# GpSimd subtracts four weight tiles at a time in place of two, from the fourth slot on

## What is computed

```python
proj = jnp.einsum('bsd,de->bse', h.astype(w_in.dtype), w_in)              # input projections
... mixers ...
return jnp.einsum('bse,ed->bsd', mix.astype(w_out.dtype), w_out)          # output projections
return (jax.nn.silu(h @ w_gate) * (h @ w_up)) @ w_down                    # feed-forward
```

## Time and profile before

| | |
|---|---|
| runs | 1914.07, 1914.70, 1916.35 us |
| profiled execution, first to last instruction | 1915.6 us |
| TensorE busy | 1770.9 us, 92% |
| VectorE busy | 926.6 us, 48% |
| ScalarE busy | 758.6 us, 40% |
| GpSimd busy | 950.2 us, 50%, of which the splits (L2811) 813.6 us |
| mean granted TensorE clock | 0.966 of full speed |

### The profile page before, as it was taken

One profiled execution on the slowest core, in us unless ns is written; L12 is line 12 of the kernel. 1 busy time (PEld: TensorE's weight loads), 2 busy tenths in 40 slices (PEclk: granted clock), 3 DMA queues, 4 the chain that ended last, 5 costly groups with the idle time before them and its releaser, 6 DMA issues.

```text
span 1915.6 us, 20168 instructions
## 1 busy us (share of the span) xinstructions
PE 1770.9 (92%) x7526; PEld 1337.8 (70%) x7526; DVE 926.6 (48%) x1394; ACT 758.6 (40%) x1261; POOL 950.2 (50%) x1108
## 2 busy tenths in 40 slices
PE   9999989999989889789999999998889899999996
PEld 6766557677767666466888888865445678888885
DVE  2043435666836799526632413357547544032344
ACT  4264554365464324644332322343333542222231
POOL 4433124457944454024655556569124456565662
PEclk9999999999999999799999999999879999999998
DMA  5221112222102221012322332311001223333231
GB/s 201 86 64 61 33 45 87 66 67 77 56 23 88 66 77 56 2 54 89 95 94 97 100 99 93 97 54 55 11 12 33 67 69 96 99 99 98 90 99 66
DMA packets 39697, 139.90 MB, mean 73 GB/s; under 512 B 4528, under 2 KB 4656, under 8 KB 39472
## 3 DMA queue, kind: packets, MB, share of 16 engines
q1 hardware_dynamic: 39600, 138.61, 22.6%
HBM read 136.50 MB, written 2.10 MB: 72 GB/s over the span
## 4 chain that ended last, share of the span: by engine, by line
PE 76%; DVE 11%; ACT 7%; POOL 3%; issue 2%; DMA 0%; SPq 0%; ACTq 0%; DVEq 0%; POOLq 0%
PE ps L643 18%; PE ps L645 17%; PE ps L644 17%; DVE ps L1882 2%; PE ps L706 2%; PE ps L683 2%; POOL wl L2811 2%; PE ps L685 2%; PE ps L684 2%; PE ps L663 1%; PE ps L669 1%; PE ps L660 1%; PE ps L1281 1%; PE ps L959 1%; ACT wh L741 1%
## 5 line engine op out<-in xcount | busy, mean ns | idle before, releaser
L2811 POOL TENSOR_TENSOR wl<-raw,wh 128x256 fp32r<-128x256 f32 x988 | 813.6, 854 | 842.0 <-ACT wh L741 836.3
L741 ACT ACTIVATE wh<-raw 128x1024 fp32r<-128x1024 f32 x246 | 259.9, 1057 | 559.2 <-PE ps L645 499.8
L643 PE MATMUL ps<-hh,wh 128*128 128x512 f32 x1068 | 437.2, 409 | 13.7 <-POOL wl L2811 3.6
L645 PE MATMUL ps<-hh,wl 128*128 128x512 f32 x1068 | 418.7, 392 | 0.0
L644 PE MATMUL ps<-hl,wh 128*128 128x512 f32 x1068 | 418.6, 392 | 0.0
L643 PE MATMUL ps<-mh,wh 128*128 128x512 f32 x632 | 261.7, 414 | 19.2 <-DVE ml L1910 4.0
L643 PEld LDWEIGHTS ps<-hh,wh 128*128 128x128 f32 x1068 | 202.4, 190 | 71.7 <-issue 13.6
L645 PE MATMUL ps<-mh,wl 128*128 128x512 f32 x632 | 250.4, 396 | 0.0
L644 PE MATMUL ps<-ml,wh 128*128 128x512 f32 x632 | 250.0, 396 | 0.0
L644 PEld LDWEIGHTS ps<-hl,wh 128*128 128x128 f32 x1068 | 202.7, 190 | 45.6 <-issue 6.0
L645 PEld LDWEIGHTS ps<-hh,wl 128*128 128x128 f32 x1068 | 202.0, 189 | 43.0
(11 more groups left out here) (477 smaller groups left out, 2443.2 us busy)
## 6 DMA issues: line engine op xcount, KB each, us to landing
raw<-in_w SPq DMA_DIRECT2D x246, 512.0 KB, 3.5
x<-in_x SPq DMA_DIRECT2D x8, 256.0 KB, 7.5
out<-x SPq DMA_DIRECT2D x8, 256.0 KB, 2.0
arena<-in_rope SPq DMA_DIRECT2D x3, 512.0 KB, 3.9
arena<-in_dec SPq DMA_DIRECT2D x1, 1024.0 KB, 7.7
mats<-in_mats SPq DMA_DIRECT2D x1, 576.0 KB, 8.5
raw<-in_w SPq DMA_DIRECT2D x2, 256.0 KB, 3.8
arena<-in_lw SPq DMA_DIRECT2D x1, 512.0 KB, 4.0
```

The source lines that it names most:

```text
L643: e.matmul(ps[b][:], a, xh, start=first, stop=False)
L645: e.matmul(ps[b][:], l, xh, start=False, stop=final).then_inc(pe.sem, pe.up(*step))
L741: e.activation(wh[:, n % NHL, :], raw[:, n % NRAW, :], ACT.Copy).then_inc(rounded.sem, rounded.up(n))
L2811: e.tensor_tensor(wl[:, n % NHL, cut(i, 2)], raw[:, n % NRAW, cut(i, 2)], wh[:, n % NHL, cut(i, 2)].bitcast(F32), SUB).then_inc(split.sem, ...
```

## The change

The first three slots stay as they were. From slot 3 on, GpSimd forms a slot's low part in two subtractions over four tiles each (128x512), and whoever waits for a part waits before tile 0 and tile 4.

```diff
+def parts_of(n):
+
+    return 2 if n < NHL else 4
...
-            elif i % 2 == 0:
-                e.wait_ge(split.sem, split["wl", n] if i + 2 == SLOT else split["part", n, i])
+            elif i % parts_of(n) == 0:
+                e.wait_ge(split.sem, split["wl", n] if i + parts_of(n) == SLOT else split["part", n, i])
...
-                if i % 2 == 0 or (k, g) == (KT - 1, gs[-1]):
-                    e.wait_ge(split.sem, split["wl", n] if i + 2 >= SLOT or (k, g) == (KT - 1, gs[-1]) else split["part", n, i])
+                if i % parts_of(n) == 0 or (k, g) == (KT - 1, gs[-1]):
+                    whole = i + parts_of(n) >= SLOT or (k, g) == (KT - 1, gs[-1])
+                    e.wait_ge(split.sem, split["wl", n] if whole else split["part", n, i])
...
-            for i in range(0, SLOT, 2):
+            many = parts_of(n)
+            for i in range(0, SLOT, many):
                 if n == 0 and i == SLOT // 2:
                     e.wait_ge(rounded.sem, rounded[0])
-                e.tensor_tensor(wl[:, n % NHL, cut(i, 2)], raw[:, n % NRAW, cut(i, 2)], wh[:, n % NHL, cut(i, 2)].bitcast(F32),
-                                SUB).then_inc(split.sem, split.up("wl", n) if i + 2 == SLOT else split.up("part", n, i))
+                e.tensor_tensor(wl[:, n % NHL, cut(i, many)], raw[:, n % NRAW, cut(i, many)],
+                                wh[:, n % NHL, cut(i, many)].bitcast(F32),
+                                SUB).then_inc(split.sem, split.up("wl", n) if i + many == SLOT else split.up("part", n, i))
```

## The result

| | before | after |
|---|---|---|
| runs beside each other | 1914.38 us (1912.23 to 1916.35, 4 runs) | 1932.87 us (1929.68 to 1937.39, 4 runs) |
| ratio after : before, 95% interval | | 1.010 (1.008 to 1.012) |
| profiled execution, span | 1915.6 us | 1935.6 us |
| VectorE busy | 926.6 us | 1002.2 us |
| GpSimd busy | 950.2 us | 836.4 us |

The kernel became 18.5 us slower, outside the predicted range, whose upper end was 1923. The profiled execution of after, 1937.39 us, is the slowest of its four runs, 4.5 us above their median; stretches of that trace add up to 20 us of loss, not 18.5. The four runs of after had mean granted clocks from 0.961 (the slowest) to 0.967 (the fastest, 1929.68), so the lower clock in the table can't be all of it: at 0.967 after is still some 15 us slower.

A forecast was written before the change was run, and what follows sets the result against it. TensorE, busy 92% of the span, was taken to bound the kernel, hiding most split work. Losses of 6.8 us less gains of 2.2 gave +4.6 on 1915.6, so 1920.2, given as 1919 for the runs' median; 8-in-10 range 1911 to 1923.

The forecast's parts named there:

- The price of a meeting: Wherever a VectorE instruction meets a GpSimd split: 0.55 us more wait behind 512 elements than behind 256.
- The wait at 1306: End of GpSimd's unbroken splits and angles, 1269.7 to 1306.1: TensorE's 1.04 us wait for the last slot disappears, -1.0 us.
- The one at 432: TensorE's 0.46 us wait at 432.3 for a slot's first part, now four tiles: +0.5 us, to near 0.9.
- a slow 512: Rival: a 512-element subtraction is slower or holds more than its like, up to 1.45 us; 1923 us, chance 0.05.
- Losses: 6.8 us: Sum of the VectorE delays priced on the chain: 1.65 + 0.7 + 1.3 + 1.1 + 0.8 + 1.2 us.
- 437.3: Slot split in turns with VectorE's scans, TensorE waiting 3.08 us for it: split 4.81 to 3.7 us, so -1.1 us.
- 353.9: Three L1372 beside two slots' splits, TensorE waiting for the last: each waits for 512 elements, +1.65 us.
- 367.9: Three L1372 beside one slot: two meet a long subtraction, the third meets none, +0.7 us.
- 507.6: L1460 at 507.6 and 518 to 521 waits 0.55 us more, one neighbour 0.4, then another 0.4: +1.3 us together.
- 1746.1: L2106 and L2108 at the end of a third of ffn1: +0.4 us, the same again at 1861, +0.8 in all.
- The meetings even out: Rival: fewer, longer VectorE waits with the same total; losses 2.2 against gains 2.2, 1915 us, chance 0.27.
- Fewer meetings win: Rival: VectorE pays per GpSimd instruction met, if a long one holds it under 0.85 us; 1909 us, chance 0.13.

The follow-up runs named there:

- fills: The kernel after, with each GpSimd subtraction replaced by a fill of the same piece with zeros: 1888.79 us, ratio 0.9876 to before.
- coarse waits alone: The kernel before, its two-tile subtractions kept, with TensorE waiting only before tiles 0 and 4 from slot 3 on: 1912.11 us, ratio 1.0000.

## Why the prediction was wrong

**The price of a meeting was right.** The same three VectorE instructions at 353 us, by what GpSimd does beside them:

| GpSimd beside them | three L1372, us | wait of each that is held |
|---|---|---|
| fills, no reads | 2.33 | 0 |
| 128 elements | 2.56 | 0.08 |
| 256 (before) | 3.37 | 0.35 |
| 512 (after) | 4.99 | 0.89 |
| 1024 | 6.28 | 2.0 (two of three) |

From 256 to 512 that is 0.54 us per meeting, where the prediction had 0.55. Its lines on this all came: three L1372 in 4.99 (5.0), a slot in 2.54 (2.5), a subtraction of 512 elements 1260 ns at its shortest (1240 to 1280). At the opening of ssm, VectorE's timeline of after gives

```profile
1411.31 1.37 DVE L2582 TENSOR_SCALAR hh_scratch<-hh_scratch 128x512 f32<-128x512 f32 x1
1412.72 1.63 DVE L2585 TENSOR_TENSOR hh_scratch<-hh_scratch,arena 128x512 f32<-128x512 f32 x1
```

for what was 0.83 and 1.09 and was to be 1.4 and 1.6. VectorE's lines by themselves, too:

```profile
L2114 DVE TENSOR_TENSOR arena<-arena x44: 691/1666/1666, 921.8 to 1880.4; 128x512 f32<-128x512 f32 x44
```

Its median was to be 1.6 us or 0.69, and is 1.67; that it is held in most of its 44 instances costs nothing, since nobody waits for it soon. Two things in the prediction's account of it are off without changing the price. It says that a VectorE instruction waits for the GpSimd one in progress; what it waits is 0.36 us less than that one takes by itself (last section). And L1494 and L1496, which it sets beside a rule on two-input instructions, have one tile and a column of scalars as inputs, so they are no case of that rule.

**GpSimd's side was right, but for one wait.** The wait at 1306 is gone (1276 to 1306 is 1.1 us shorter, forecast 1.0). The one at 442 fell from 3.08 to 1.51 (forecast near 2); in part that is scatter, since two kernels with before's subtractions there have it at 1.7. The one at 432 was to grow from 0.46 to 0.9 and stayed at 0.46; in its place the same kind of wait one slot earlier, at 424.5, which the prediction had counted even, grew from 3.12 to 3.67. Of 1.25 us for 512 elements and two-input reads, nothing is to be taken back; "a slow 512" is out.

**The step that failed is the count of the losses**, the list that ends in "Losses: 6.8 us". It priced VectorE instructions that were already on the chain of before. It left out those beside the chain that had little slack, which come onto it once they are late. By place, forecast against measured: slots 52 to 55, -1.1 against +6.7; slots 41 to 44, +2.4 against +5.95; slots 164 to 178, +1.0 against +4.8.

- *437.3, "-1.1".* The largest error, and in sign. GpSimd's gain was there, but the scans behind it, in the same turns with GpSimd, had 1.85 us of slack and became 5.0 later. By themselves these four slots cost 6.7 us, not -1.1. The prediction's sentence on "two turns fewer" counted what the turns cost GpSimd, and not VectorE.
- *353.9 and 367.9, "+1.65" and "+0.7".* 2.4 forecast; slots 41 to 44 alone cost 5.95. At 353.9 L1372 went from 3.37 to 4.99, +1.6, as forecast. At 367.9 it went from 3.59 to 5.21, also +1.6 and not +0.7: the third was to meet nothing, and meets GpSimd's own 512-element L1661 (L1667). Before, GpSimd came to L1661 at 372.05, when the third L1372 was over; now the slot's split takes it 2.98 us in place of 4.15, and it comes sooner:

```profile
367.87 2.98 POOL L2818 TENSOR_TENSOR wl<-raw,wh 128x512 fp32r<-128x512 f32 x2 [9.47 <-ACT wh L747]
370.81 1.71 POOL L1667 TENSOR_TENSOR arena<-arena 128x512 f32<-128x512 f32 x1
```

  Together 3.2 us, and this is what TensorE's two waits (L1264) grew by, from 2.6 to 5.8 us, in after and in the kernel with these four slots alone. In the latter the stretch 336 to 374 took 41.5 us, so 3.2 more than before. The other 1.6 of after's 43.1 are matmuls behind the second wait at the lower clock level. The rest up to the median of 5.95 can lie in the scatter of before: two kernels with its code there take 36.7 to 36.8 us in place of 38.3.
- *1259 to 1498.* Priced at L2576 and L2579, +1.1, with three single meetings (1440, 1490, 1491.6) at some 0.3 each, against the queue gain of 1.0. Measured +4.8 for the 15 slots. The chain of before ran through GpSimd's queue at the opening of ssm, so VectorE's L792, L795 and L806 (L798, L801 and L812 in after), which normalise the input beside it, were not looked at. VectorE's timeline of after:

```profile
1279.59 1.82 DVE L798 SCALAR_TENSOR_TENSOR arena<-arena,vec,nrm 128x512 f32<-128x512 f32 x1
1281.44 1.64 DVE L801 TENSOR_TENSOR x<-x,arena 128x512 f32<-128x512 f32 x1
1283.00 1.53 DVE L812 SCALAR_TENSOR_TENSOR hl<-x,vec,hh 128x512 fp32r<-128x512 f32 x1
```

  The first two were 1.22 and 1.11 us long. TensorE's waits for them at the opening, before (1255 to 1278 us):

```profile
PE ps L663 <- DVE hl L806: 1.8, 3, 0.7
```

  After (1262 to 1288):

```profile
PE ps L668 <- DVE hl L812: 3.6, 3, 1.8
```

  They doubled, by 1.8 us, most of the 2.5 that 1263 to 1276 lost. The kernel with four tiles in these 15 slots alone has the same 3.6. Behind 1324 its trace is 5.1 us longer than that of before, of which L2576 and L2579 are 1.1; the rest wasn't traced to instructions.
- *Everything else* (507.6, 518, 1746.1, 1861, 754.6): forecast 1.3 + 0.8 + 0.3, less 0.6, so some +1.8; measured +1.3 (-0.4 to +3.1). No fault to be seen there.

**The rivals.** "The meetings even out" would have left the time at 1915, and the places where only two or three instructions meet a slot went against it. "Fewer meetings win" fell at its own condition: a long one holds VectorE for 0.89 to 0.91 us, over 0.85.

**What stays open.** The stretch 1306 to 1324 took 22.6 us in after and 17.9 before, and this isn't the longer subtractions in it: the kernel with four tiles in slots 164 to 178 has them there, too, and took 17.7. Kernels with subtractions of two tiles there took 17.9 (three of them) and 20.6 (coarse waits alone), so it varies without them. In after 1.4 us of it are a wait of TensorE for VectorE (L2502) that before doesn't have and coarse waits alone has, and the rest are matmuls at the lower clock level. A window's row of before (window, us, then busy us of TensorE, weight load, VectorE, ScalarE and GpSimd with their instructions, the granted clock, and the share and GB/s of the transfers):

```profile
1306.20:1324.10 17.90, 17.12 (x62) 9.93 (x62) 13.12 (x15) 5.10 (x9) 17.67 (x17) 0.90 0.27 89
```

The same stretch of after:

```profile
1317.80:1340.40 22.60, 20.46 (x65) 11.65 (x63) 16.02 (x17) 6.08 (x9) 22.29 (x18) 0.77 0.23 70
```

The clock was 0.90 and is 0.77, and TensorE is 3.3 us longer busy with nearly the same matmuls. Over the whole run the clock stood at its lower level for 153.6 us in place of 133.4, and TensorE was busy in 117.8 of these, before in 96.8. So the extra time at the lower level was mostly matmuls that ran slower, not waits, and the page has it too: 1783.4 us of TensorE in place of 1770.9 for the same 7526 matmuls. Part of the loss therefore reached the kernel by way of the clock. In the odd stage the lower level stands right behind waits of TensorE: in before behind those of 1.9 us at 357, 3.1 at 424 and 3.1 at 442, in after also behind the 2.3 us at 373 and the 4.1 at 456. That speaks for the clock following the waits. No run set it by itself, so how many of the 18.5 us it carries stays open.

## What to carry to other kernels

An engine's busy time that will grow by contention must be followed everywhere, not only on the chain of waits: for each place where TensorE will need a result of the held engine, take its slack, the time from when it is ready to when it is wanted. What the delay exceeds of that is a new wait. One trace can flatter the slack: the scan at 449 had 1.85 us of it where TensorE's matmuls before it ran at the lower clock level, and 0.22 to 0.25 us in three traces with the same subtractions where they didn't. Two-input GpSimd instructions beside a VectorE that is nearly late should be short (256 elements and not 512 here; under 256 no kernel became measurably faster); where nobody is near to waiting, their length is free, and making them shorter than need be only feeds GpSimd's own queue. A change of this kind is first judged by how much longer the untouched engine is busy, then by which of it anybody waits for.

## What the hardware showed that was not expected

- A VectorE instruction with only one full tile as input is held up too: L1450 (a tile and a column of scalars) takes 1.65 and 1.44 us beside splits of 512 elements, where it takes 0.53 alone. In before one of its two at this place (445.93) came during splits of 256 and took only 0.55, so it isn't held each time. L1342, which reads one tile from PSUM and one from SBUF, takes 0.68 us at 357.19, with the last of four splits beside it, and 0.66 to 0.69 in all of its 20 instances, beside GpSimd or not.
- The splits' contention with VectorE costs this kernel no more than 23.7 us in all, though VectorE alone spends 101.6 of its 926.6 us on it: the fills show both.
- GpSimd's instructions of 128, 256, 512 and 1024 elements take 444, 712, 1253 (L1661) and 2401 ns, and hold L1372 for 0.08, 0.35, 0.89 and 2.0 us. That is their own time less 0.36 us each time, near enough (0.08, 0.35, 0.89, 2.04), a description that fits four lengths; why the wait is shorter by this much, no run shows.
